# Filler matmuls at the start of a transformer layer, and its 32 experts as two inner loops with the next gate matrix loaded ahead

## What is computed

```python
g_idx = jnp.argmax(g_logits, axis=-1)                     # one of 4 groups
top_p, top_i = lax.top_k(e_prob, TOP_K)                   # 2 of its 8 experts
...
def expert_block(args):
    rt, rg, e = args                                      # rows of this block, gates, expert
    xb = x_pad[rt]
    hb = jax.nn.silu(xb @ w_gate[e]) * (xb @ w_up[e])     # 2048 -> 512
    return (hb @ w_down[e]) * rg[:, None]                 # 512 -> 2048
```

## Time and profile before

| what | value |
|---|---|
| median of 3 runs | 1521.53 us (1520.55 to 1521.89) |
| profiled execution, its own time | 1520.34 us |
| its span from first to last instruction | 1518.4 us |
| TensorE busy | 1343.2 us, 88% |
| VectorE busy | 590.5 us, 39% |
| ScalarE busy | 347.6 us, 23% |
| bytes moved | 473.91 MB, mean 312 GB/s |

### The profile page before, as it was taken

The page is one execution under the profiler, slowest core; times in us unless marked ns, Lnnn a source line. Parts: engine busy times, 40 slices in busy tenths (PEclk is TensorE's granted clock), DMA queues, the critical chain, the costliest instruction groups (busy, mean ns, idle before and its releaser), DMA issues.

```text
span 1518.4 us, 22122 instructions
## 1 busy us (share of the span) xinstructions
PE 1343.2 (88%) x8510; PEld 714.2 (47%) x8511; DVE 590.5 (39%) x1175; ACT 347.6 (23%) x595; POOL 32.4 (2%) x41
## 2 busy tenths in 40 slices
PE   6999999999999999787888888888889988888885
PEld 4989999566666663232222222322323322232221
DVE  4335444044574443242243234224324422332344
ACT  5332322123453322111111111111212111111113
POOL 1000000000000000000000000000000000000000
PEclk9999999999999989999898888988989989898887
DMA  9454451023353368999999999999989999999994
GB/s 324 131 166 137 161 167 61 10 70 111 92 180 112 131 285 355 408 432 430 432 433 432 429 433 433 431 429 433 433 369 400 432 434 432 428 434 432 432 428 180
DMA packets 69751, 473.91 MB, mean 312 GB/s; under 512 B 9532, under 2 KB 46656, under 8 KB 55824
## 3 DMA queue, kind: packets, MB, share of 16 engines
q1 hardware_dynamic: 68640, 470.78, 76.0%
q0 software_dynamic: 832, 2.48, 0.4%
q10 hardware_dynamic: 240, 0.09, 0.0%
HBM read 469.97 MB, written 3.38 MB: 312 GB/s over the span
## 4 chain that ended last, share of the span: by engine, by line
PE 52%; DMA 41%; DVE 3%; issue 2%; ACT 1%; DVEq 0%; SPq 0%; ACTq 0%
DMA ring<-in_w_down 41%; PE ps L888 11%; PE ps L587 5%; PE ps L588 5%; PE ps L589 5%; PE ps L873 3%; PE ps L649 2%; PE ps L676 2%; PE ps L739 2%; PE ps L740 2%; PE ps L741 2%; PE ps L752 2%; PE ps L850 2%; PE ps L670 1%; PE ps L879 1%
## 5 line engine op out<-in xcount | busy, mean ns | idle before, releaser
L1566 DVE TENSOR_TENSOR hreg<-ps,hreg 128x512 f32<-128x512 f32 (+1 forms) x396 | 239.4, 677 | 291.6 <-PE ps L899 291.6
L873 PE MATMUL ps<-ring,mix 128*32 128x512 f32 x2112 | 278.4, 675 | 31.7 <-DMA ring<-in_w_up 19.5
L888 PE MATMUL ps<-ring,mix 128*32 128x512 f32 x1056 | 165.7, 784 | 62.5 <-DMA ring<-in_w_down 54.7
L899 PE MATMUL ps<-mix 32*128 32x512 f32 (+1 forms) x792 | 156.3, 612 | 26.4 <-ACT mix L1249 25.6
L1206 ACT COPY mix<-ps 128x512 f32<-128x512 f32 x66 | 70.5, 1068 | 446.4 <-PE ps L873 446.4
L873 PEld LDWEIGHTS ps<-ring,mix 128*32 128x32 f32 x2112 | 74.5, 121 | 206.3 <-issue 176.2
L587 PE MATMUL ps<-xT_hi,w_hi 128*128 128x320 f32 (+1 forms) x528 | 165.6, 314 | 2.9 <-DVE w_lo L1301 2.9
L588 PE MATMUL ps<-xT_lo,w_hi 128*128 128x320 f32 (+1 forms) x528 | 164.6, 312 | 0.0
L589 PE MATMUL ps<-xT_hi,w_lo 128*128 128x320 f32 (+1 forms) x528 | 164.5, 312 | 0.0
L1301 DVE TENSOR_TENSOR w_lo<-ring,w_hi 128x1024 fp32r<-128x1024 f32 (+1 forms) x66 | 76.8, 1204 | 110.5 <-ACT w_hi L1019 110.5
L888 PEld LDWEIGHTS ps<-ring,mix 128*32 128x32 f32 x1056 | 39.6, 138 | 162.7 <-issue 104.4
(11 more groups left out here) (258 smaller groups left out, 1186.5 us busy)
## 6 DMA issues: line engine op xcount, KB each, us to landing
ring<-in_w_gate SPq DMA_DIRECT2D x31, 4096.0 KB, 22.2
ring<-in_w_up SPq DMA_DIRECT2D x31, 4096.0 KB, 23.7
ring<-in_w_down SPq DMA_DIRECT2D x31, 4096.0 KB, 23.7
ring<-in_w_in SPq DMA_DIRECT2D x32, 1024.0 KB, 8.2
ring<-in_w_o SPq DMA_DIRECT2D x16, 1024.0 KB, 6.7
ring<-in_w_up SPq DMA_DIRECT2D x2, 2048.0 KB, 11.7
ring<-in_w_gate SPq DMA_DIRECT2D x2, 2048.0 KB, 8.4
ring<-in_w_down SPq DMA_DIRECT2D x2, 2048.0 KB, 22.3
```

The source lines that it names most:

```text
L873: last = pe.matmul(ps[r:r + B, bank, :], x[:, k % 4, k // 4, :], w[:, k, :], start=k < 4, stop=k >= KC - 4)
L888: last = pe.matmul(ps[B * j:B * (j + 1), 4, :], h[:, c, :], w[:, c, 512 * j:512 * j + 512], start=c == 0, stop=c == 3)
L899: pe.matmul(ps[0:tn, COMB_BANKS[u % 8], :], gates[r, t0:t0 + tn], rows[r, :], start=True, stop=True).then_inc(full_sem, 1)
L1566: dve.tensor_tensor(h, ps[0:tn, COMB_BANKS[u % 8], :], h, ALU.add).then_inc(signal, 1)
```

## The change

1. **Filler at the start.** TensorE multiplies `ones` by `ones` (128x128x128, float32, into a bank nobody reads): 28 times before the first transpose, 10 times between tile 0 and tile 1, 7 times ahead of tile 2, and once ahead of each of the chunks 6 to 15.
2. **Loads of the routing stage.** `late_loads` issues the gain and the tokens first and the router weights behind them; these go to `krt` and `const`. VectorE scales the router weights one step later.
3. **Experts.** `extra_blocks`, its buffers and the expert ahead of the loop go. Each expert is two inner loops over its blocks: the first does gate, gather, fold, transpose, up, fold; the second transposes the gates, does down and `combine`. The halves of a hidden block are kept in `hTs`, and ScalarE copies the one in turn to `hT`. The outer loop takes two experts at a time.
4. **Transfers.** A second place for a gate matrix, `gate_b`, lies over `mix`, `ckv` and a piece of `cq`, which are free by then. Odd experts use it, even ones ring slots 0 and 1. The gate of expert 1 is loaded when the routing stage has read these (`hg_ready`), ahead of the wait for the tables. In the loop the order is gate of e+1, up of e, down of e.
5. **End.** The gate of expert 31 is loaded behind the down of expert 30, the down of expert 31 comes as four transfers of 1 MB, and TensorE waits for each by itself. The final gain is loaded into ring slot 0 behind the last of them.

```diff
+            def warm(count):
+                for _ in range(count):
+                    pe.matmul(ps[:, SSQ_BANK, 0:P], ones[:, :], ones[:, :], start=True, stop=True)
+            pe.wait_ge(s_ones, 1)
+            warm(28)
...
             for i in range(2):
+                if i:
+                    warm(10)
                 pe.wait_ge(x_scaled, i + 1)
...
+            warm(7)
             pe.wait_ge(x_scaled, 3)
             for c in range(KC):
                 if c >= RB:
+                    warm(1)
                     claim(pe, f"xt{c}")
...
-            sp.wait_ge(routed, 4)
-            with sp.Fori(1, NE) as e:
-                used = sp.value_load(tables[0:1, 3, bass.ds(e, 1)], min_val=1, max_val=65)
-                for m in range(3):
-                    sp.wait_ge(weights_used, e * 3 + (m + 1 - 3))
-                    sp.wait_ge(extra_used[m], used)
...
+            sp.wait_ge(hg_ready, 12)
+            sp.dma_start(gate_b[:, :], rows_of(0, a["w_gate"][0, 1])).then_inc(gate_b_full, 16)
+            sp.wait_ge(routed, 2)
...
+            with sp.Fori(1, NE - 3, 2) as e:
+                before = blocks_before(e)
+                load_gate(e + 1, before, gate_a, slot_full[0])
+                load_up(e, before)
+                load_down(e, before)
+                before = blocks_before(e + 1)
+                load_gate(e + 2, before, gate_b[:, :], gate_b_full)
+                load_up(e + 1, before)
+                load_down(e + 1, before)
...
+            load_down(NE - 2, before)
+            load_gate(NE - 1, before, gate_b[:, :], gate_b_full)
+            before = blocks_before(NE - 1)
+            load_up(NE - 1, before)
+            sp.wait_ge(down_done, before)
+            for c in range(4):
+                sp.dma_start(ring[:, 4 + c // 2, D * (c % 2):D * (c % 2 + 1)],
+                             rows_of(2, a["w_down"][0, NE - 1])[:, D * c:D * (c + 1)]).then_inc(down_last[c - 1] if c else slot_full[4], 16)
...
-            pool.wait_ge(hg_ready, 12)
-            pool.dma_start(gain, a["norm_final"].rearrange("(a d) -> a d", a=1).to_broadcast([P, D])).then_inc(s_gfin, 16)
+            pool.wait_ge(down_last[2], 17)
+            pool.dma_start(gain_last, a["norm_final"].rearrange("(a d) -> a d", a=1).to_broadcast([P, D])).then_inc(s_gfin, 16)
...
+            def expert(e, odd):
+                first = pe.value_load(tables[0:1, 0, bass.ds(e, 1)], min_val=0, max_val=NE + 20)
+                count = pe.value_load(tables[0:1, 1, bass.ds(e, 1)], min_val=1, max_val=MAXB)
+                with pe.Fori(0, count) as k:
+                    it = first + k
+                    pe.wait_ge(xg_ready, it + 1)
+                    pe.wait_ge(comb_added, first * 12 + 7)
+                    gate_full(e, odd)
+                    gate_or_up(xg, 0, odd, 2).then_inc(gate_done, 1)
+                    pe.wait_ge(comb_added, first * 12 + 8)
+                    pe.wait_ge(pick_ready, it + 2)
+                    gather(pickr, 0, gathered)
+                    pe.wait_ge(h_copied, it * 2 + 1)
+                    pe.wait_ge(hT_ready, it + 1)
+                    fold(0).then_inc(folded, 1)
+                    pe.wait_ge(g_copied, it + 2)
+                    pe.wait_ge(comb_added, first * 12 + 12)
+                    gathered_T(gsb, 1, transposed)
+                    matrix_full(1, e)
+                    gate_or_up(xg, 1, odd, 4).then_inc(up_done, 1)
+                    pe.wait_ge(h_copied, it * 2 + 2)
+                    pe.wait_ge(silu_ready, it + 1)
+                    fold(1).then_inc(folded, 1)
+                tail = pe.value_load(tables[0:1, 2, bass.ds(e, 1)], min_val=0, max_val=16)
+                after = first + count
+                with pe.Fori(0, count) as k:
+                    it = first + k
+                    pe.wait_ge(hT_ready, after + 1)
+                    pe.wait_ge(comb_added, it * 12 + 5)
+                    pe.wait_ge(gates_ready, it + 1)
+                    gates_T(gpick, gt_full)
+                    pe.wait_ge(comb_added, it * 12 + 6)
+                    pe.wait_ge(h_picked, it + 1)
+                    down(hT, e, tail + 1).then_inc(down_done, 1)
+                    pe.wait_ge(xg_ready, after + 1)
+                    pe.wait_ge(gt_copied, it + 1)
+                    pe.wait_ge(y_copied, it + 1)
+                    pe.wait_ge(comb_added, it * 12 + 12)
+                    combine(gT, yb, comb_full, comb_added, it * 12 + 12)
...
+                    act.wait_ge(up_done, it + 1)
+                    copy_xT(xg, 1, transposed, it + 2, xg_ready)
+                    copy_half(1, 4, h_copied)
...
+                    act.wait_ge(hT_ready, after + 1)
+                    act.copy(hT, hTs[:, bass.ds(k, 1), :].rearrange("p b q -> p (b q)")).then_inc(h_picked, 1)
```

369 lines of the change are left out of this document (145 added, 224 removed).

## The result

| | kernel before | changed kernel |
|---|---|---|
| time, median | 1520.6 us | 1528.3 us |
| ratio to before, 95% interval | | 1.0048 (1.0038 to 1.0057) |
| profiled execution, time | 1520.34 us | 1529.35 us |
| span | 1518.4 us | 1527.2 us |

The change makes the kernel slower by half a per cent, where 12.4 us less were forecast. One of the changed kernel's 14 executions was a slow one of 3167.35 us; the ratio leaves it out, and it moves the median by less than 0.1 us. Timed again, beside the experiments, the changed kernel took 1531.3 us, ratio 1.007 (1.0057 to 1.0083).

The account below looks back on a forecast made before the run. TensorE bounds up to 545 us, then bytes over 432 GB/s plus transfer stops and the tail. 7.0 + 2.4 + 2.4 - 1.1 + 2.7 - 1.0 = 12.4 us off gives 1509.1 us, range 1500 to 1516.

Parts of the forecast that it names:

- Term 1: Start: fillers among the transposes make everything up to 545 us 1.0 us late, bounds 2.1 early and 3.5 late.
- Term 2: Routing loads: issued later, from about 424 us, but hidden by the output projection; cost nothing.
- Term 3: Stop at the tables: early gate of expert 1 wins 7.0 us, the final gain's bytes moved away 2.4.
- Term 4: First experts: of 4.4 us of stops 2.0 are left, bounds 0 and 4.4; gain 2.4 us.
- Term 5: Steady expert: TensorE's cycle settles at 27 to 29 us, under the 29.1 of its transfers; cost 0, thin cover.
- Term 6: Expert with two blocks: transfers stop 9.5 us, bounds 6.5 and 11, against 8.4 before; loss 1.1 us.
- Term 7: End: down of expert 31, loaded in quarters, finishes sooner behind the last landing; gain 2.7 us, range 1.7 to 4.
- the rivals: Better bounds everywhere, 1502 us (0.15); no two-block stop, 1499.6 (0.05); TensorE-bound, slower (0.08); start loses more, 1515.5 (0.12).
- the slower one: Expert loop: TensorE's cycle above 29.1 us becomes the bound, or jumps back refetch code, then 1582 us; chance 0.08.

Follow-up runs that it names:

- gate_late: Changed kernel with the gate of expert 1 loaded behind the gate product of expert 0 instead of ahead of the tables; 1536.8 us, ratio to before 1.0112.
- before_longer5: Kernel before with five matmuls of 512 columns on constants added in each expert, transfers unchanged; 1524.9 us, ratio 1.0031.
- order_only: Changed kernel with row transposes behind up, ScalarE's half-block copy first, gate transposes not waiting for the hidden rows; 1521.8 us, ratio to before 1.0004.
- short_cycle: Changed kernel with reordered transposes and ScalarE copy, one wait dropped, and bank 2 fifth in the combination; 1522.3 us, ratio to before 1.0004.
- end_order: Changed kernel with the gate of expert 31 loaded ahead of up and down of expert 30; 1530.9 us, ratio to before 1.0055.

## Why the prediction was wrong

It forecast 1509.1 us (12.4 less) with a range from 1500 to 1516; it is 1528.3. Term by term, by the two spans:

- **Term 1, the start**: forecast 1.0 us late, bounds 2.1 early and 3.5 late. 4.8 late at the first projection (31.91 instead of 27.10), 5.8 at 549.55 us in this trace, some 2 at that point in the mean of all traces, 3.3 over the timed runs without and with fillers. The step that failed is "VectorE's copies take 0.47 us each": the last ten chunks go at TensorE's pace, a filler and the transposes of three tiles, 0.84 us. That the first projection then runs at full rate was right and gives a part back. The ten fillers took 4.45 us, not 3.5, at a granted clock of 0.52:

```profile
15.60 4.45 PE L592 MATMUL ps<-ones 128*128 128x128 f32 x20
...
24.36 0.49 PE L592 MATMUL ps<-ones 128*128 128x128 f32 x2
24.68 0.38 PE L603 MATMUL ps<-const,mix 128*128 128x128 f32 x2
24.99 0.27 PE L603 MATMUL ps<-const,work 64*128 64x64 f32 x1
25.19 0.49 PE L592 MATMUL ps<-ones 128*128 128x128 f32 x2
```

- **Term 2**: nothing, and nothing was seen.
- **Terms 3 and 4, the tables and the first experts**: forecast 11.8 us won, 10.6 by the windows, and `gate_late` loses 5 to 8 of them again. Term 3 was right (7.9 against 7.0; the 2.4 of the final gain's bytes is worked out in both and timed in no run). Term 4 came only in part: of its 2.4 this trace shows 0.3. The wait without a releaser ahead of down has gone, but this execution's router stage is slower, and the gate of expert 2 is issued only at 581.52 us. In the second trace of the changed kernel that gate is issued at 573.85 us and 574 to 700 us loses 0.3 us instead of 4.1, which is more than term 4 had.
- **Term 5, the steady expert**: the cycle was forecast at 27 to 29 us and its cost at nothing. The cycle is 27.4 to 28 where nothing holds TensorE, and between 640 and 1110 us it costs nothing. The failed step is "cost 0": the cover is there only while transfers run and the next landing is a full 29.1 us away. That a longer chain under the transfers costs is shown on both kernels, 4.3 us in `before_longer5` and 7 to 9 by `order_only`; how it divides over the stops and the end is known only in part.
- **Term 6, the expert with two blocks**: forecast a stop of 9.5 us, bounds 6.5 and 11; 14.6 in this trace, 13 to 19 in others. The times were on the safe side: gate issued 30.0 us behind the down product before (forecast 32.5), first down 41.5 (47.9), second ending at 56.7 (57.1). What was off is the step from them to the stop. By windows of 2 us the two pieces are 6.3 and 7.1 us with their ramps, where 5.1 and 5.7 were worked out, and the gate at 1178.95 us leaves a third of 1.1; and then 9.5 was taken instead of the sum of 10.8. One part of it the working had left out: from the issue at 1141.22 us to the first bytes is 1.0 us, and in the kernel before, behind the issue at 1136.40, it is as long. The first down was 6.4 us earlier than forecast, and the stop came out longer all the same. The chain's length has little part in it (`short_cycle`).
- **Term 7, the end**: forecast 2.7 us won, 7.8 lost, the largest miss. The failed step is "by the cycle of term 5 it is ready about at the last landing". With the gate a transfer ahead there are only five matrices between the landings of down 29 and down 31, 49.0 us, and TensorE needs 56.7 for its two cycles. The order of the loads doesn't change it (`end_order`).

The sum by the spans is 5.8 - 11.3 + 6.5 + 7.8 = 8.8 us, with 11.3 as what the sum needs. None of the rivals was it: the slower one expected a cycle above 29.1 us in the steady loop or code fetched in it, and neither is there (three down landings in a row lie 29.1 apart from 876 to 1051 us, and no code packets in the loop). A chance of 0.08 for slower left out the case that each gain in the loads is paid for by TensorE's chain and by a longer stop at the two-block expert. What of the two-block stop comes from the second block's gather and folds inside the expert, and what from both downs standing behind both first halves, is read from the trace alone; a version in which the second down stands ahead of the first combination was not tried.

## What to carry to other kernels

A chain that hides under the transfers is hidden only while they run. Before making it longer by 4 us for a prefetch, look at the places where transfers stop and above all at the last stage: a load ahead takes just as much out of the last intervals between landings as it moved forward, and the chain must fit in what is left. Here 49.0 us were left for 56.7. Where a chain is hidden, its order still matters: moving the transposes and one copy and dropping one wait won 7 to 9 us, as much as the prefetch did, and with the fillers left out it is the only version of the whole computation here below the kernel before (0.9985, and the interval reaches 0.9998). Fillers that keep the clock up on the critical path have to be cheaper than what they save at the lower clock.

## What the runs showed of the hardware

- Waits without a releaser in the first passes of TensorE's expert code come and go with edits far away: 0.97 and 6.46 us in the kernel before, 5.43 and 5.57 with fillers some 550 us earlier, 3.11 in one place with five more matmuls in the body, none with nine. A packet of 16 KB on the `instruction` queue lies some 2.6 us ahead of the end of all seven of 0.9 us and more, so this is very likely code arriving; what sets the packet's time is open. It costs up to 9 us of transfers.
- ScalarE's two table loads per pass (1.28 us each) came from nesting the loops and went with a single silu ahead of them; they were hidden in both cases.
- The router stage's clock takes different courses in kernels that are the same up to there. The granted clock from 545 to 566 us was 0.68 in the first trace of the changed kernel and 0.92 in the second, 0.76 in others, and the gate of expert 2 is issued 32.0 us behind the down halves in the first and 28.4 in the second.
- The first bytes of a transfer into an idle queue come 1.0 us behind its issue (1141.22 us in the changed kernel; 1136.40 in the kernel before, seen in windows of 0.1 us and less).
